# Gathers of own expert rows moved among the cell writes, and the first load of own activations moved behind the gates

## The reference

```python
def peer_ffn(xn, w_q, sub_keys, u, v):       # u, v: 16384 experts x 2048
    q = (xf @ w_q).reshape(n, PEER_HEADS, 2, PEER_DK // 2)
    s = einsum('nhpd,hpkd->nhpk', q, sub_keys)
    ...                                       # top 16 of 128 x 128 per head, 8 heads
    g = softmax(tv)                           # gates of the 128 picked experts
    act = gelu(einsum('nd,ned->ne', xt, u[it]), approximate=False) * gt
    return einsum('ne,ned->nd', act, v[it])
```

## Time and profile before

| | us |
|---|---|
| median of 3 runs | 2030.02 |
| lowest and highest run | 2023.45, 2034.09 |
| span of the profiled execution | 2021.1 |
| PE busy in it | 1971.8 |
| DVE busy in it | 1526.5 |
| POOL busy in it | 711.9 |

### The profile page before, as it was taken

The page is one execution under the profiler, slowest core; times in us unless marked ns, Lnnn a source line. Parts: engine busy times, 40 slices in busy tenths (PEclk is TensorE's granted clock), DMA queues, the critical chain, the costliest instruction groups (busy, mean ns, idle before and its releaser), DMA issues. The chain is left out here.

```text
span 2021.1 us, 29296 instructions
## 1 busy us (share of the span) xinstructions
PE 1971.8 (98%) x11128; PEld 1755.7 (87%) x11128; DVE 1526.5 (76%) x2291; ACT 863.2 (43%) x873; POOL 711.9 (35%) x488
## 2 busy tenths in 40 slices
PE   6999998999999999999999999999999999999998
PEld 6997776999999999989999999988888888888886
DVE  4988755456688898888888898567777767777786
ACT  4340136335535555445454555433343343334343
POOL 2010110220336687888868783010111001113320
PEclk9999998999999999999999999999999999999999
DMA  5464294344434777878788887889998898999984
GB/s 209 165 194 140 96 393 170 133 166 146 146 128 148 265 264 275 274 269 293 263 294 271 313 311 288 305 307 358 342 343 327 324 347 343 353 371 347 370 314 148
DMA packets 101226, 531.27 MB, mean 263 GB/s; under 512 B 19376, under 2 KB 21568, under 8 KB 45792
## 3 DMA queue, kind: packets, MB, share of 16 engines
q1 hardware_dynamic: 71552, 408.93, 56.5%
q0 software_dynamic: 24304, 106.45, 14.4%
q10 hardware_dynamic: 5296, 14.98, 1.9%
HBM read 491.34 MB, written 38.14 MB: 262 GB/s over the span
## 5 line engine op out<-in xcount | busy, mean ns | idle before, releaser
L912 DVE TENSOR_TENSOR wl<-raw,wh 128x2048 fp32r<-128x2048 f32 x310 | 710.9, 2294 | 281.9 <-ACT wh L535 281.3
L535 ACT ACTIVATE wh<-raw 128x2048 fp32r<-128x2048 f32 x310 | 593.1, 1915 | 583.0 <-DMA raw<-in_v 408.6
L1587 PE MATMUL acc<-xhl,wh 128*128 128x448 f32 x2048 | 646.2, 376 | 9.9 <-DVE wl L912 9.9
L1588 PE MATMUL acc<-xhl,wl 128*128 128x224 f32 x2048 | 542.2, 265 | 0.0
L1587 PEld LDWEIGHTS acc<-xhl,wh 128*128 128x128 f32 x2048 | 385.3, 188 | 41.9 <-DVE wl L912 12.1
L1588 PEld LDWEIGHTS acc<-xhl,wl 128*128 128x128 f32 x2048 | 392.1, 191 | 0.0
L2089 POOL DMA_INDIRECT G<-gsum,cell x224 | 355.7, 1588 | 83.2 <-issue 71.6
L1564 PE MATMUL acc<-xhl,wh 128*128 128x288 f32 x768 | 231.0, 301 | 15.4 <-DVE wl L948 14.4
L1565 PE MATMUL acc<-xhl,wh 128*128 128x288 f32 x768 | 227.9, 297 | 0.0
L1566 PE MATMUL acc<-xhl,wl 128*128 128x288 f32 x768 | 227.5, 296 | 0.0
L1564 PEld LDWEIGHTS acc<-xhl,wh 128*128 128x128 f32 x768 | 146.0, 190 | 18.3 <-DVE wl L948 14.4
(11 more groups left out here) (323 smaller groups left out, 2584.5 us busy)
## 6 DMA issues: line engine op xcount, KB each, us to landing
raw<-in_u SPq DMA_DIRECT2D x128, 1024.0 KB, 5.6
raw<-in_v SPq DMA_DIRECT2D x128, 1024.0 KB, 5.1
raw<-in_w_mix SPq DMA_DIRECT2D x28, 1024.0 KB, 4.8
G<-zero SPq DMA_DIRECT2D x16, 1024.0 KB, 13.9
raw<-in_w_out SPq DMA_DIRECT2D x16, 1024.0 KB, 4.8
raw<-in_w_pq SPq DMA_DIRECT2D x16, 1024.0 KB, 4.8
gin<-G SPq DMA_DIRECT2D x32, 512.0 KB, 9.1
h<-hbg ACTq DMA_DIRECT2D x32, 448.0 KB, 5.1
```

The source lines that it names most:

```text
L535: act.activation(wh[:, n % 4], raw[:, n % 4], ACT.Copy).then_inc(hi_done, 1)
L912: dve.tensor_tensor(wl[:, n % 4], raw[:, n % 4], wh[:, n % 4].bitcast(F32), ALU.subtract).then_inc(lo_done, 1)
L1587: pe.matmul(acc[:, s, 0:2 * NU], wh[:, s, j, :], xu[:, j, 0:2 * NU], start=(j == 0), stop=False)
L1588: ins = pe.matmul(acc[:, s, 0:NU], wl[:, s, j, :], xuh[:, j, :], start=False, stop=(j == DT - 1))
```

## The change

The table moves own gathers 4 to 9 and 26 to 28 to earlier scatters. The sixth group of own results (`own_hidden(5)`) is no longer written right after the last pair but behind gather 29, and gather 30 goes between the sixth and the seventh group; before, it came behind the seventh. The load of `hin_a` becomes a step of its own: for the first block it and the wait for own results come after the second half of the gates. In the v stage's loop its place stays.

```diff
-A_PICKS = {(1, 2): {0: (0, 1)}, (1, 3): {14: (2,)}, (0, 0): {10: (3,)}, (0, 1): {6: (4,)}, (1, 4): {0: (5,), 11: (6,)},
-           (1, 5): {3: (7,), 15: (8,)}, (0, 2): {0: (9,), 5: (10,)}, (0, 3): {0: (11,), 9: (12,)}, (1, 6): {0: (13,), 11: (14,)},
+A_PICKS = {(1, 2): {0: (0, 1)}, (1, 3): {14: (2,)}, (0, 0): {10: (3,)}, (0, 1): {0: (4,), 10: (5,)}, (1, 4): {4: (6,), 12: (7,)},
+           (1, 5): {0: (8,), 12: (9,)}, (0, 2): {5: (10,)}, (0, 3): {0: (11,), 9: (12,)}, (1, 6): {0: (13,), 11: (14,)},
...
-           (0, 6): {0: (21,), 4: (22,), 9: (23,), 14: (24,)}, (0, 7): {0: (25,), 5: (26,), 9: (27,), 14: (28,)}}
-A_CELLS = {(1, 4): 0, (0, 2): 1, (1, 6): 2, (0, 4): 3, (0, 6): 4, (0, 7): 5}
+           (0, 6): {0: (21,), 4: (22,), 9: (23,), 14: (24,)}, (0, 7): {0: (25,), 4: (26,), 8: (27,), 12: (28,)}}
+A_CELLS = {(1, 4): 0, (0, 2): 1, (1, 6): 2, (0, 4): 3, (0, 6): 4}
...
                 sp.dma_start(hin[:, 4 * a:4 * a + 4, :], dr["h"][2 * b + a]).then_inc(hg_in, 16)
-                if a == 1:
-                    sp.dma_start(hin_a[:], hidden_a[b]).then_inc(hg_in, 16)
+
+            def load_own_hidden(b):
+
+                sp.dma_start(hin_a[:], hidden_a[b]).then_inc(hg_in, 16)
...
                 if n == 121:
                     sp.wait_ge(h_out, 32)
                     sp.wait_ge(routed, 1)
-                    sp.wait_ge(h_a_out, 16 * PICKS_A)
                     load_hidden(0, 0)
...
                 if n == 124:
                     load_gates(0, 1)
+                    sp.wait_ge(h_a_out, 16 * PICKS_A)
+                    load_own_hidden(0)
...
                     if s % 8 in (2, 3):
                         load_hidden(b + 1, s % 8 - 2)
+                    if s % 8 == 3:
+                        load_own_hidden(b + 1)
...
             own_pick(29)
+            own_hidden(5)
+            own_pick(30)
             own_hidden(6)
-            own_pick(30)
             own_pick(31)
             own_hidden(7)
```

## The result

The changed kernel takes 2011.05 us in the median of 4 runs (2008.33 to 2013.99), the kernel before 2027.65 us in 4 runs of its own (2023.45 to 2034.09). The ratio is 0.9919, with a 95% interval from 0.9898 to 0.9940.

The account below looks back on a forecast made before the run. PE, busy 1971.8 of 2021.1 us, was taken to bound the kernel. Terms 6.64 + 2.21 + 1.2 = 10.05 us, 10.4 with longer first matmuls, gave 2030.02 - 10.4 = 2019.6 us; range 2012 to 2028.

Parts of the forecast that it names:

- I take the same distance: Whole kernel: the runs' median stays 8.9 us above the profiled span, so 10.4 us come off 2030.02.
- gathers 26 to 30: End of u stage: DVE's waits at products 29 and 30 go, PE gains 2.21 us, bounds 0 and 2.4.
- What bounds the kernel, and where: PE, busy 1971.8 of 2021.1 us; its u-stage waits on `wl`, 9.9 us, come from late gathers and a load.
- Gathers 4 to 9: Ahead of slot 45: gather 8 issued at 842.6; PE's 4.03 us wait and the slow clock go, 6.64 us.
- The load: Ahead of slot 123: load lands 3.4 us earlier, PE's 1.51 us wait shrinks; term 1.2 us, bounds -0.7 and 1.51.
- plus 2.21 because PE now gets there earlier: Slot 123: PE's earlier arrival raises what the load must gain from 1.51 to 3.7 us.
- Rival 1: DMA transfers bound slot 123's load: PE's wait grows from 1.51 to about 2.9 us; time 2022.6, chance 0.20.
- The small waits: u stage: PE's four other waits, 2.15 us together, stay, as DVE is late with its own work.
- rival 2: u stage: first gain given back to other, hidden waits on `wl`; about 3 us left, time 2027, chance 0.13.
- rivals 3, 4 and 5: Gather 30 stays late, 2021.9, 0.08; gather 8 held by buffer, 2026.5, 0.05; SP's moved wait stops PE, 2033 and more, 0.07.
- signs of being wrong: Changed profile: PE wait over 4 us somewhere new, ACT over 7 us for slot 123's load, SP stopped before slot 125.
- The rule against it: POOL's gathers, 0.97 to 3.10 us: DVE and GpSimd shut each other out, so gathers beside busy DVE are long.

Follow-up runs that it names:

- e1_late: Kernel before with only gathers 26 to 30 and the sixth group's writing at their new places: 2019.76 us against 2027.19, ratio 0.9968.
- second trace of before: The kernel before run once more, unchanged, for another trace: 2026.23 us, span 2024.4.
- the seven traces of the table: Traces with the old gather order up to gather 7: two of the kernel before, five of edited kernels; u stages 652.5 to 667.4 us.

## Why the prediction was wrong

The time came out 8.55 us under the forecast. 7.1 of them are one step, "I take the same distance", and that is the step that failed; 1.45 are in the sum itself, whose term for gathers 26 to 30 was too small. The steps in the order of the prediction:

**What bounds the kernel, and where: right.** The waits named in the trace were the ones to go, and the chain from a gather through DVE's `wl` to PE is confirmed from both sides, by gather 8 put later and by scatters left out. The sum for the span, 2010.7, was met by 2010.0.

**Gathers 4 to 9: mechanism right, size probably too small.** The term was 6.64 us; alone they gave 9.2 (0.9953), with an interval that still holds 6.64. "So DVE's 5.54 us and the 0.9 us go" came true, but it took the waits of one execution for the waits of the kernel. Products 4 to 6, which showed no wait, stood on the edge of one. In another execution of the same program they waited 4.2 us, with product 7's 2.34 on top. The sum allowed nothing for such near waits.

**Gathers 26 to 30: mechanism right, size wrong.** The term was 2.21 us with a bound of 2.4. In most other executions of the old order the same place cost more: product 30 waited 1.22, 2.93, 3.60, 6.53, 7.41 and 8.00 us where the first trace had 2.45, and behind PE's longer waits the clock fell here too (below). Alone this part gave 7.4 us in the medians, ratio 0.9968, with the bound of 2.4 outside the interval. The geometry was right: less the 6.5 us by which all moved up, gathers 29 and 30 came 9.1 and 8.0 us earlier, where I had 9.35 and 7.2, and that was enough for the longer waits too.

**The load: about right.** From issue to landing the load of slot 123 took 2.46 us less, I had 3.4; the wait of 1.51 us is gone. Wrong was the sentence "plus 2.21 because PE now gets there earlier". The load leaves when slot 119 is done, so it moves up with PE: without the last part, with PE early, the wait was 1.21 and 1.45 us and not 3.7. Rival 1 falls with it.

**The small waits: wrong in the good direction.** "The four small waits stay": 1.2 us of waits are left, in place of 2.15.

**The step from span to time: the one that put the number outside the range.** "I take the same distance", 8.9 us between the profiled span and the runs' median, was taken for a fixed part around the span. Measured, that part is 1.8 us in every run. Of the other 7.1 us, 4.7 are that the profiled execution was shorter than the median of the four runs, so that the others lose more somewhere; 2.4 are that the median of three runs, 2030.02, lay that much above the median of four, which is chance. With a 1.8 us distance the sum's span gives 2012.5, within 1.5 us of the measured 2011.05. It comes so near because the change removes the waits whatever their length, so that the changed kernel's span could be had from the good execution; the gain could not.

**Chances.** The scatter of the runs was counted as noise that blurs the gain. It was in part the loss itself: the standard deviation is 4.5 us in the 26 runs before and 2.6 in the 6 runs after; with gathers 4 to 9 alone moved it is 4.1, with 26 to 30 alone 1.9. Neither rival 1 nor rival 2 (given back) nor rivals 3, 4 and 5 came in: no new place had a wait of over 0.7 us, gather 8 was issued at 846.71, and SP met the own results complete. One of the signs of being wrong did show, ACT idle for over 7 us ahead of the load of slot 123 (8.31), and it was badly chosen: that idle time did not reach PE.

**The rule against it: its mechanism is in the traces, and it did no harm.** "Nothing in the rows says why one is long" holds for the rows, not for the trace. These are DVE's rows beside gather 8 (870.80, 2.24 us long) and gather 29 (1214.29, 2.14 us) of the earlier trace rows:

```profile
869.91 2.28 DVE L912 TENSOR_TENSOR wl<-raw,wh 128x2048 fp32r<-128x2048 f32 x1
...
1213.29 2.29 DVE L912 TENSOR_TENSOR wl<-raw,wh 128x2048 fp32r<-128x2048 f32 x1
```

Both gathers started while DVE formed a `wl` and ended 0.85 us behind it. In the u stage of the first trace 146 gathers and scatters started during a `wl` or an own product, and 139 of these took over 1.5 us, each ending 0.83 to 0.87 us behind DVE's operation. Of the 149 others only 2 did; most took 0.96 us. The other traces show the same. DVE's operations keep their 2.3 us, so it is POOL alone that is held up. For the change it made no difference: gather 29 took 1.93 us and gather 30, beside short operations of DVE, 0.98.

## What to carry to other kernels

Before adding up waits, compare the profiled execution's span with the runs: a distance larger than what other executions show around their spans says that the profile is one of the better executions (or the few runs were bad ones), and that the waits in it may be less than what a change can remove. Where an engine with a fixed pace takes data from one whose pace varies, count the places with little in hand as losses too; a transfer that comes just in time in one trace is late in the next.

## What the runs showed of the hardware

In all traces the granted clock fell behind every wait of PE in the u stage of 2.49 us and more, and behind none of up to 1.95 us; in e1_late it also fell behind one of 2.15 us just after the stage. In the second trace of before, the stretch behind the wait of 4.65 us and the one around and behind that of 3.28 us:

```profile
885.00:890.00 5.00, 4.42 (x15) 4.12 (x16) 4.86 (x6) 0.14 (x1) 4.08 (x4) 0.50 0.63 215
1247.00:1252.00 5.00, 4.13 (x18) 3.86 (x19) 4.97 (x6) 0.61 (x1) 0.00 (x0) 0.73 0.38 157
```

Behind the first PE ran at once at 1.2 GHz, in the second the fall came within the slot. At slot 45 the price was 1.5 to 2.6 us for waits of 3.35, 4.03, 4.46, 4.65 and 8.36 us, with no order in it, so in these five traces it hardly depends on the wait's length. One behind a wait of 2.49 us cost 1.7 us; this stretch is from the trace with gather 8 put later:

```profile
1234.00:1237.00 3.00, 3.00 (x14) 2.81 (x15) 2.61 (x2) 2.08 (x2) 0.71 (x1) 0.72 1.02 421
```

POOL's stretch of some 90 scatters and gathers took 177.4 to 182.7 us with the same instructions in the seven traces of the table, by its own durations (143.0 to 145.2 us busy) and by two idle stretches ahead of new pairs (6.4 to 9.5 us together). Some 41 of the 94 operations in it are held up by a `wl` or a product of DVE; over 0.96 us each, that comes to 52.3 us in the first trace and 54.6 in the longest stretch. So the few us by which POOL is late lie beside some 50 that it spends behind DVE; no run here moves POOL's operations out of DVE's way. What makes the two idle stretches longer or shorter stays open. So does the start of the u stage, which lies anywhere from 644.9 to 650.2 us in these traces, and the part behind slot 127's start, 713.9 to 718.0 us; both are parts of the scatter that is left.
